# Output and down projections of a four-layer network: three 256-column matmuls per weight block become one of 512 columns and one of 256

## The reference

```python
# first kind, twice
h = h + merged @ w_o[layer]
u = rms_norm(h, norm_ffn_g[layer])
h = h + conv_glu(u, ..., w_down)      # hidden (256 x 2816) @ w_down (2816 x 1024)
# second kind, twice
x = x + mix @ w_out
h2 = rms_norm_2(x, g_mlp_norm)
x = x + jnp.square(jax.nn.relu(h2 @ w_up)) @ w_down      # (256 x 4096) @ (4096 x 1024)
```

## Time and profile before

| | |
|---|---|
| median of 3 runs | 1983.94 us |
| lowest and highest of them | 1979.28 and 1986.15 us |
| the profiled execution, its own time | 1983.01 us |
| its span, first to last instruction | 1981.2 us |
| TensorE granted clock, mean over the span | 0.96 of full speed |
| HBM read | 267.52 MB |

### The profile page before, as it was taken

How to read it: one execution, slowest core, us unless ns; L and a number is a source line. 1 busy time by engine, 2 the same in 40 slices (tenths; PEclk the granted TensorE clock), 3 DMA queues, 4 the chain that set the end, 5 groups by cost and what they waited for, 6 DMA issues and landing times.

```text
span 1981.2 us, 43199 instructions
## 1 busy us (share of the span) xinstructions
PE 1869.6 (94%) x15850; PEld 1742.0 (88%) x15850; DVE 1317.3 (66%) x1956; ACT 1082.4 (55%) x1862; POOL 923.7 (47%) x662
## 2 busy tenths in 40 slices
PE   9988889999999988989999999987999999879999
PEld 9968779999999968879999999865999997669999
DVE  4677725669955587735669964676886527768754
ACT  5653455557655643455457664646555446365543
POOL 5732449929986633359929985521000044120000
PEclk9999989999999999899999999977999999779999
DMA  7522015656666522015556665320566653116664
GB/s 244 155 87 65 13 35 168 176 155 186 187 206 176 158 86 71 23 40 169 176 155 186 187 195 169 112 80 17 164 186 201 186 157 116 59 38 171 187 186 144
DMA packets 146917, 271.13 MB, mean 137 GB/s; under 512 B 16433, under 2 KB 16946, under 8 KB 146738
## 3 DMA queue, kind: packets, MB, share of 16 engines
q1 hardware_dynamic: 145296, 264.97, 45.8%
q10 hardware_dynamic: 1442, 3.66, 0.5%
HBM read 267.52 MB, written 1.05 MB: 136 GB/s over the span
## 4 chain that ended last, share of the span: by engine, by line
PE 66%; DVE 19%; POOL 7%; ACT 6%; issue 2%; DVEq 0%; DMA 0%; ACTq 0%
PE bank L669 66%; POOL ring_split L1361 7%; ACT arena L1395 5%; DVE arena L1957 1%; DVE arena L1956 1%; PE bank L811 1%; DVE ring_split L2075 1%; DVE arena L2537 1%; DVE arena L2144 1%; DVE arena L2518 1%; DVE arena L2294 0%; DVE arena L2559 0%; ACT hi_ring L1395 0%; DVE arena L2191 0%; DVE arena L2597 0%
## 5 line engine op out<-in xcount | busy, mean ns | idle before, releaser
L1361 POOL TENSOR_TENSOR ring_split<-ring,hi_ring 128x512 fp32r<-128x512 f32 x602 | 856.1, 1457 | 742.0 <-ACT hi_ring L1395 741.4
L1395 ACT ACTIVATE hi_ring<-ring 128x512 fp32r<-128x512 f32 x890 | 537.5, 628 | 410.3 <-PE bank L669 388.4
L669 PE MATMUL bank<-u_hi,hi_ring 128*128 128x256 f32 (+1 forms) x2160 | 615.6, 285 | 6.8 <-POOL ring_split L1361 6.6
L669 PE MATMUL bank<-u_split,hi_ring 128*128 128x256 f32 (+1 forms) x2160 | 607.9, 281 | 0.0
L669 PE MATMUL bank<-u_hi,ring_split 128*128 128x256 f32 (+1 forms) x2160 | 607.0, 281 | 0.0
L669 PEld LDWEIGHTS bank<-u_hi,hi_ring 128*128 128x128 f32 (+1 forms) x2160 | 407.0, 188 | 13.5 <-POOL ring_split L1361 6.8
L669 PEld LDWEIGHTS bank<-u_split,hi_ring 128*128 128x128 f32 (+1 forms) x2160 | 406.8, 188 | 1.7
L669 PEld LDWEIGHTS bank<-u_hi,ring_split 128*128 128x128 f32 (+1 forms) x2160 | 406.3, 188 | 1.0
L669 PE MATMUL bank<-arena 64*64 64x64 f32 (+6 forms) x3680 | 240.7, 256 | 27.4 <-DVE arena L2191 18.6
L669 PEld LDWEIGHTS bank<-arena 64*64 64x64 f32 (+3 forms) x3680 | 210.3, 156 | 63.3 <-issue 39.6
L2075 DVE TENSOR_TENSOR ring_split<-ring,hi_ring 128x512 fp32r<-128x512 f32 x288 | 196.5, 712 | 93.1 <-ACT hi_ring L1395 90.4
(11 more groups left out here) (265 smaller groups left out, 2522.3 us busy)
## 6 DMA issues: line engine op xcount, KB each, us to landing
ring<-in_stream SPq DMA_DIRECT2D x1002, 256.0 KB, 2.7
par<-in_params ACTq DMA_DIRECT2D x3, 637.0 KB, 4.1
h<-in_x SPq DMA_DIRECT2D x4, 256.0 KB, 4.1
cst<-in_cst SPq DMA_DIRECT2D x1, 993.0 KB
out<-h ACTq DMA_DIRECT2D x3, 256.0 KB, 2.6
par<-in_params ACTq DMA_DIRECT2D x1, 633.0 KB, 8.5
out<-h ACTq DMA_DIRECT2D x2, 128.0 KB, 2.2
msk<-in_masks SPq DMA_DIRECT2D x1, 104.0 KB
```

Of the source, the lines that this page charges most:

```text
L669: ins = nc.tensor.matmul(o, l, r, start=start, stop=stop)
L1361: G.tensor_tensor(ring_lo[:, c, :], ring[:, c, :], hi_ring[:, s % HI_RING, :].bitcast(F32), ALU.subtract).then_inc(lo_by_pool, 1)
L1395: return nc.scalar.activation(o, i, f, **kw)
```

## The change

For the output and the down projections of all four layers the two matmuls with the high weights become one: its moving operand is 512 columns wide, the 256 of the high and the 256 of the low activations (`Parts.both`, a view of two stretches of memory), and it fills a whole bank with two partial sums. The low weights x high activations go on as a matmul of 256 columns into one half of that bank. Each output tile now has a bank of its own (8 groups instead of 5), and `add_last` adds the two halves of a bank to `h` one after the other, two additions of 256 columns for each tile. The low parts of the weights of the first kind's down projection, all but its first 32 blocks, go from GpSimd to VectorE (name "D" in `BY_VECTOR1`). Arithmetic, weights and the order of the stream are the same.

```diff
-SIZES1 += [("WO", 64), ("U first", 16), ("U second", 16)] + [(f"U{i}", 16) for i in range(2, 22)] + [("D", 176)]
+SIZES1 += [("WO", 64), ("U first", 16), ("U second", 16)] + [(f"U{i}", 16) for i in range(2, 22)] + [("D first", 32), ("D", 144)]
...
-BY_VECTOR1 = {"WO"}
+BY_VECTOR1 = {"WO", "D"}
 BY_VECTOR2 = {"WO", "D"} | {f"U{i}" for i in range(2, 16)}
...
+class Parts:
+
+
+    def __init__(self, hi, lo, span, hi_at, lo_at):
+        self.hi, self.lo, self.span = hi, lo, span
+        self.at, self.step, self.high = min(hi_at, lo_at), abs(hi_at - lo_at), int(hi_at > lo_at) * T
+
+    def both(self, k):
+
+        rows = self.span[:, :].ap[0]
+        return bass.AP(tensor=self.span, offset=self.at + k * T, ap=[list(rows), [self.step, 2], [1, T]])
...
-LAST_WO, LAST_D = (tuple(n + j for j in ("0", "1", "2", "3", "3b")) for n in ("WO", "D"))
+LAST_WO, LAST_D = (tuple(f"{n}{j}" for j in range(KD)) for n in ("WO", "D"))
 PARTS = (slice(0, 2), slice(2, 4), slice(4, 6), slice(6, 7), slice(7, 8))
...
-    g += [*LAST_WO, "U0", "U1", "norm2"] + [f"U{i}" for i in range(2, 22)] + ["D0"] + ["positions"] * last + [*LAST_D[1:]]
+    g += [*LAST_WO, "U0", "U1", "norm2"] + [f"U{i}" for i in range(2, 22)] + [*LAST_D[:2]] + ["positions"] * last + [*LAST_D[2:]]
...
+        def twins(name, hi, lo, n):
+
+            first, last = min(hi.offset, lo.offset), max(hi.offset, lo.offset)
+            span = nc.alloc_sbuf_tensor_at(name, [P, last - first + n * T], F32R, offset=arena_at + 4 * first)
+            at = [ap.offset - first for ap in (hi, lo)]
+            views = [v3(span[:, a:a + n * T], n) for a in at]
+            return Parts(*views, span, *at)
...
-        hidden_hi, hidden_lo = v3(twin("hidden_hi", arena[:, fv.at + 4 * T:fv.at + 36 * T]), 32), v3(twin("hidden_lo", hidden), 32)
+        hidden_parts = twins("hidden_parts", arena[:, fv.at + 4 * T:fv.at + 36 * T], arena[:, 0:32 * T], 32)
+        hidden_hi, hidden_lo = hidden_parts.hi, hidden_parts.lo
...
+        merged_parts = twins("merged_parts", arena[:, nn_at:nn_at + 2048], merged, KD)
+        merged_hi, merged_lo = (a.rearrange("p a t -> p (a t)") for a in (merged_parts.hi, merged_parts.lo))
...
+        mix_parts = twins("mix_parts", sq2, mix, 8)
+        mix_hi, mix_lo = mix_parts.hi, mix_parts.lo
...
+                def pair(bank, w, act, k, start, stop, full=None):
+
+                    low = lambda: mm(bank[:, act.high:act.high + T], w[1], act.hi[:, k, :], False, False)
+                    if not stop:
+                        mm(v3(bank[:, :], 2), w[0], act.both(k), start, False)
+                        low()
+                    else:
+                        low()
+                        mm(v3(bank[:, :], 2), w[0], act.both(k), start, stop, full=full)
+
+                def project_pairs(names, act, K_, ready=None, warm=0):
+
+                    for i, name in enumerate(names):
+                        bank = B.open(pe, name)
+                        keep_warm(bank, 0 if i else warm)
+                        q = W.take(name, K_)
+                        for k in range(K_):
+                            if ready and i == 0:
+                                ready(k)
+                            pair(bank, W.block(q + k), act, k, k == 0, k == K_ - 1, full=name if k == K_ - 1 else None)
+                            W.done(q + k)
...
-                def project_across(name, act, K_, ready):
-
-
-                    bank = B.open(pe, name)
-                    q = W.take(name, 2 * K_)
+                def project_across(names, act, K_, ready):
+
+
+                    open_ = [B.open(pe, name) for name in names]
+                    q = W.take(names[0], 2 * K_)
+                    W.ends[names[1]] = W.ends[names[0]]
                     for k in range(K_):
                         ready(k)
                         for i in range(2):
-                            mm3(bank[:, i * T:(i + 1) * T], W.block(q + 2 * k + i), cut(act, k), (k, i) == (0, 0), (k, i) == (K_ - 1, 1),
-                                full=name if (k, i) == (K_ - 1, 1) else None)
+                            pair(open_[i], W.block(q + 2 * k + i), act, k, k == 0, k == K_ - 1, full=names[i] if k == K_ - 1 else None)
                             W.done(q + 2 * k + i)
...
-                for j, (name, part_) in enumerate(zip(LAST_WO, PARTS)):
-                    project(name, part_.stop - part_.start, (v3(merged_hi, KD), v3(merged_lo, KD)), ready=None if j else after("merged_ready", 0, 2), warm=0 if j else 8)
+                project_pairs(LAST_WO, merged_parts, KD, ready=after("merged_ready", 0, 2), warm=8)
...
-                for j, (name, part_) in enumerate(zip(LAST_D, PARTS)):
-                    if j == 0:
-                        project_across(name, (hidden_hi, hidden_lo), 22, after("hidden_ready", 0, 1))
-                    else:
-                        project(name, part_.stop - part_.start, (hidden_hi, hidden_lo), 22)
-                    if last and j == 0:
-                        bank = B.open(pe, "positions")
-                        pe.wait_ge(S["ready"], past["ready"] + 1)
-                        mm(bank[:, 0:T], ones[0:1, :], t512[0:1, 0:T], full="positions")
+                project_across(LAST_D[:2], hidden_parts, 22, after("hidden_ready", 0, 1))
+                if last:
+                    bank = B.open(pe, "positions")
+                    pe.wait_ge(S["ready"], past["ready"] + 1)
+                    mm(bank[:, 0:T], ones[0:1, :], t512[0:1, 0:T], full="positions")
+                project_pairs(LAST_D[2:], hidden_parts, 22)
...
-                    for j, (name, part_) in enumerate(zip(LAST_WO, PARTS)):
-                        bank = B.open(pe, name) if half == 0 else banks[B.slot[name][0]]
-                        tiles = part_.stop - part_.start
-                        for i in range(tiles):
-                            q = W.take(name if half else name + " attention", 4)
-                            for k in range(4):
-                                if i == 0 and j == 0:
-                                    mix_in(k)
-
-                                mm3(bank[:, i * T:(i + 1) * T], W.block(q + k), cut((mix_hi, mix_lo), 4 * half + k), half == 0 and (i, k) == (0, 0),
-                                    (half, i, k) == (1, tiles - 1, 3), full=name if (half, i, k) == (1, tiles - 1, 3) else None)
-                                W.done(q + k)
+                    for i, name in enumerate(LAST_WO):
+                        bank = banks[B.slot[name][0]] if half else B.open(pe, name)
+                        q = W.take(name if half else name + " attention", 4)
+                        for k in range(4):
+                            if i == 0:
+                                mix_in(k)
+                            last = half == 1 and k == 3
+                            pair(bank, W.block(q + k), mix_parts, 4 * half + k, half == 0 and k == 0, last, full=name if last else None)
+                            W.done(q + k)
...
-                for j, (name, part_) in enumerate(zip(LAST_D, PARTS)):
-                    project(name, part_.stop - part_.start, (hidden_hi, hidden_lo), 32, ready=None if j else after("hidden_ready", 0, 2))
+                project_pairs(LAST_D, hidden_parts, 32, ready=after("hidden_ready", 0, 2))
...
-                for j, (name, part_) in enumerate(zip(names, PARTS)):
-                    hi.upto(name, HI_RING if j < 3 else LEAD)
+                for j, part_ in enumerate(PARTS):
+                    hi.upto(names[part_.stop - 1], HI_RING if j < 3 else LEAD)
                     act.wait_ge(S["h_ready"], past["h_ready"] + fresh + j + 1)
                     C.link(A(dst[:, part_, :], h[:, part_, :], ACT.Square), S["squares_ready"])
...
             def add_last(C, B, names, dst, which, sums=True, last=False):
-                for j, (name, part_) in enumerate(zip(names, PARTS)):
-                    lo.upto(name)
-                    bank = B.wait(dve, name)
+                for j, part_ in enumerate(PARTS):
+                    own = names[part_]
+                    lo.upto(own[-1])
                     if last and j == 0:
                         dve.wait_ge(params_in, (layers[0] + 1) * 16)
                         C.link(V.tensor_tensor(gains, PAR2.of(par, "g_final"), PAR2.of(par, "g_mix"), ALU.mult))
-                    o = h[:, part_, :].rearrange("p a t -> p (a t)")
-                    C.link(V.tensor_tensor(o, o, bank[:, 0:(part_.stop - part_.start) * T], ALU.add), S["h_ready"])
-                    B.release(dve, name)
+                    for name, k in zip(own, range(part_.start, part_.stop)):
+                        bank = B.wait(dve, name)
+                        for half in range(2):
+                            ins = V.tensor_tensor(h[:, k, :], h[:, k, :], bank[:, half * T:(half + 1) * T], ALU.add)
+                            C.link(ins, S["h_ready"] if half and name == own[-1] else None)
```

(1 more changed line is left out.)

10 lines of the change are left out of this document (4 added, 6 removed).

## The result

Over 12 executions of each kernel, the kernel after takes 2000.19 us in the median (1991.31 to 2005.16) and the kernel before 1982.87 (1966.39 to 1988.86). The ratio is 1.0108, with an interval of 1.0087 to 1.0130. That is some 21 us slower (the two medians lie 17 us apart), where 6.5 us faster had been forecast. It is the second rival that came, at 1999 us.

What follows compares the result with a forecast made beforehand. TensorE's train of matmuls, with short waits for VectorE, was taken as the bound. Gains of 17.6 us less 2.7 (joints), 5.0 (second-kind output projections) and 3.4 (clock) gave 6.5: from 1983.94 to 1977.4 us, range 1967 to 1989.

Steps and rivals of the forecast that it cites:

- the second rival: 512 columns cost as much as two matmuls of 256: no gain at 353.5 ns, 15 us slower, 1999 us; chance 0.14.
- the upper bound: Price of a pair: 353.5 ns, 3 x 117.9, if 512 columns cost exactly what two matmuls cost now.
- sum of gains: Second-kind down projections 11.5, first-kind output projections 2.6, first layer's down projection 1.5, second layer's 2.0: 17.6 us.
- The account of the angles: Second layer's down projection: angle making on VectorE falls from 17.9 to some 9 us, stall about 2 to 2.5 us.
- the stall rival: Third rival, second layer's down projection: angles stay at 17.9 us, stall 11.2 us instead of 2.3, 1986 us; chance 0.14.
- Joints and tails: Waits at projection ends: six joints of 0.45 us, 2.7; two second-kind output projections lose 5.0 us, plus 3.4 by clock.
- the 216: Nanoseconds between starts of plain float32 passes of 256 columns, taken as the price of one 512-column matmul.
- The boundary of 342 ns a pair: Pair price, about 342 ns, from which the second rival decides because gains and losses cancel.
- The first rival: All goes as cleanly as it can: 325 ns a pair, no loss of clock, 1968 us; chance 0.2.

Runs made afterwards that it cites:

- The widths: Kernel before with first-kind down projections streaming 64 to 512 contiguous columns per matmul; median starts 112 ns for 64 to 240 (but 160), 231 ns for 512.
- The runs of the output projections alone: Kernel after with the down projections as before, so pairs in the output projections alone; ratio to before 1.0081 (1.0051 to 1.0110).
- those of the down projections alone: Kernel after with the output projections as before, so pairs in the down projections alone; ratio to before 1.0087 (1.0059 to 1.0114).

## Why the prediction was wrong

**The step that failed** is the price of the 512-column matmul, "So a pair costs 216 and 112 to 118, and I take 331 ns". The trace has 235 and 118, together 353, which was the upper bound. I took 216 from a plain float32 pass of 256 columns because it streams for as many cycles. It shows that such a pass reaches 216; it doesn't show that a single-pass matmul does for 512 columns. The widths show what does hold: 0.446 to 0.460 ns for each column above the floor of 112 ns. I had read the excess of 113 to 118 over 107 as load and stream getting in each other's way, something a longer stream would hide. It goes with the columns, and cutting out a load saves nothing. So the gains of 11.5 (second-kind down projections) and 2.6 us (first-kind output projections) were 0.3 and 0.6, and with the first-kind down projections below the sum of gains, 17.6 us, came out as a loss of 3.2.

**First-kind down projections.** The first layer was to gain 1.5 and lost 2.3 us, by the pace: 113 before, 118 after. The second was to gain 2.0 and lost 1.8. The account of the angles held all the same. From 1172.07 to 1181.06 they took 9.0 us (9 forecast, 17.9 before), the stall is 1.5 us of idle time (1.8 by the starts), where 2 to 2.5 were forecast, and the stall rival fell. What I took for a property of the layer, "What differs between 113 and 118 ns I don't know", is one of two states, and a second look at before would have shown the other one. Against a before that runs its first layer at 118, the change would lose nothing there: the 2.3 us are in part luck of the profile.

**Joints and tails** came as worked out: 0.45 us at each of six joints; the last sum of the second-kind output projection 12.9 us behind the first addition (12.3 forecast); idle times of 3.87 and 3.52 us (4.1 forecast); half clock for 3.4 us behind the first (3.4). For the two tails 8.4 us were forecast and 9.1 came. Only the sum they were set against was missing.

**The rivals.** The second rival named what happened with its reason against it, "the 216", and got 0.14. Its two conditions, no gain at 353.5 and the first layer falling to this pace, both came true. The boundary of 342 ns a pair, "where gains and losses cancel", was miscounted: the gains shrink by 0.95 us for each nanosecond, so by the prediction's own terms the 6.5 us are gone at 338. The measured 353 lies beyond both. The range ended at 1989 because this rival was left out. Its 15 us are found in the profile. The medians are 17 apart and the ratio says 21, so 2 to 6 us are over. The runs of the output projections alone point to clock for them and those of the down projections alone don't; it stays open. That the median fell within 1.2 us of the rival's 1999 is partly luck. The first rival (325 ns a pair) fell with the 353, the third with the angles at 9.0 us.

## What to carry to other kernels

A duration from another kind of instruction is a bound and no price, however well its cycles match. With the price at either end of the bounds this change was 12 us faster or 15 slower, and the row that I leaned on was one of plain float32 passes. By the widths, merging pays below some 250 columns here, where 64 columns cost the same 112 ns as 240 (no merge of that size was run). Above that only the columns count, and whatever the merge costs on other engines (a second addition before a sum that TensorE waits for) is a pure loss. And before a pace is taken as a property of a stage, look at a second execution.

## What was not expected of the hardware

A steady train of single-pass matmuls of 256 columns, each with its own load of 128 weight columns, runs at one of two paces, 113 or 118 ns, at the same clock. It keeps it for hundreds of matmuls, and the same kernel takes one or the other in different executions. Behind one matmul issued as 128 and 128 columns the second-kind down projections ran at 113 in four traces (eight stretches; in five the starts before the mark were at 118, in the other three the last few were already at 113 to 114). Without marks two of twelve such stretches did, in the six traces of kernels with narrow matmuls. Which cut works depends on the stage, and pairs of 512 and 256 columns never left 353 ns behind 32 different marks. What in the engine makes the two paces is not settled.
